# Writing the software loops of a two-block transformer kernel out in straight lines

## The chip, the cores and the metric

One NeuronCore of one Trainium2 chip runs the whole program. The metric is the device time of one execution in microseconds (us), taken without a profile; beside it there is one profiled execution, whose trace the rows below come from.

## What is computed

The program computes a stack of three transformer blocks for one sequence of 256 tokens with model width 1024, in float32: one block with sliding-window, forgetting and latent attention and a convolved feed-forward, then two blocks (`DEPTH_2 = 2`) with adaptive modulation, one with stick-breaking and block attention and one with retention, and a final norm. The change touches how the feed-forward parts, and a few loads around them, are written. In the reference they are

```python
h = rmsnorm(x, ffn_pre_norm[l])
u = causal_depthwise_conv(h @ w_up[l], conv_w[l], conv_b[l])
gate, up = jnp.split(u, 2, axis=-1)
y = (jax.nn.gelu(gate, approximate=True) * up) @ w_down[l]
...
def ada_mod(c, w, b):
    m = jax.nn.silu(c) @ w + b
    return jnp.split(m[:, None, :], 6, axis=-1)
```

The two later blocks have the same feed-forward with silu in place of gelu and without the convolution. `ada_mod` multiplies one vector by a matrix of 1024 x 6144 in each of them; the kernel does this on VectorE.

## The kernel before

All weights come from HBM in chunks of mostly 1 MB, in the order in which TensorE needs them: 171 chunks in twelve phases. The feed-forward phases are `up` (22 chunks), `down` (11), `gu0` (22), `dn0` (16), `gu1` (22) and `dn1` (16). Each engine runs its own hand-written instruction stream, and the streams meet only at semaphores.

A chunk passes through five engines. SyncE (SP) loads it into one of four `raw` slots (L623), once `split_ready` says that the slot's last chunk was split. ScalarE (ACT) writes its high part `w_hi` (L775) and VectorE (DVE) the rest `w_lo` (L2123), two slots each, in two halves. TensorE (PE) then multiplies both parts with both parts of the activations: three matmuls for each 128 x 128 tile of weights (L1409, L1410, L1411 in `three`), so 48 matmuls of 256 columns for a chunk of `up`, `gu0` or `gu1`, and 33 for one of `dn0` or `dn1`. The products of a chunk go to one of two PSUM banks (`lin`). VectorE empties it: in `up` with the four convolution taps of a chunk (L2420), in `gu0` and `gu1` with the product of gate and up (L2444), and only then does `lin_free` let TensorE start the next chunk but one. ScalarE takes the gelu or silu before that and rounds the product afterwards (L1089), and GpSimd (POOL) makes its low part (L695, L702).

Between the chunks stand the pieces of `ada_mod`: SP loads 1 MB into one of two slots of the arena (L613), and VectorE reduces it in two passes of 128 x 1024 (L2227) and adds the bias (L2230). In `up` every second chunk has such a piece, in `gu0` each of the chunks 4 to 19.

The chunk loops go through `steps(eng, n, lead, tail, body)`. It writes out `lead` chunks, puts as many groups of four (`UNROLL = 4`) as fit into a hardware loop (`eng.Fori`), if there are at least two groups, and writes out the rest. Inside the loop everything that depends on the chunk is computed from the loop's counter: semaphore values, row addresses in HBM, columns of `cols` and `mod`. `Step.n(f)` gives a plain number outside a loop and a register expression in one. The calls give these loops (trips of four chunks):

| engine | loops |
|---|---|
| PE | `up`, `gu0`, `gu1`: 3 trips each, chunks 8 to 19; `dn0`: 3; `dn1`: 2 |
| DVE | `up`, `gu0`: 3 trips each, chunks 8 to 19; `dn0`, `dn1`: 2 each; none in `gu1` |
| ACT | `up`, `gu0`: 3 each; `gu1`, `dn0`, `dn1`: 2 each |
| POOL | `up`: 4 trips; `gu0`, `gu1`: 5 each |
| SP | `up`: 3; `qkv`, `gu0`, `dn0`: 2 each; `ret_in`: 5; `dn1`: 3 |

Of the kernel before, what the change touches and what calls it, by code (L numbers as in the profile page):

```python
# [39 lines left out]
UNROLL = 4  # L40
# [147 lines left out]

def steps(eng, n, lead, tail, body):

    lead = min(lead, n)
    trips = (n - lead - tail) // UNROLL
    if trips < 2:
        trips = 0
    for c in range(lead):
        body(Step(c))
    if trips:
        with eng.Fori(0, trips) as i:
            for j in range(UNROLL):
                body(Step(lead + j, i))  # L200
    for c in range(lead + trips * UNROLL, n):
        body(Step(c))


# [81 lines left out]
def build(nc, dram):  # L286
    ctx = ExitStack()
    with ctx:
# [311 lines left out]
        def _(sp):  # L600
# [25 lines left out]
            def phase(ph):  # L626
                load = weights_of(ph)

                def one(step):
                    load(step)  # L630
                    if ph.name == "w_in" and step.j == 1:
                        sp.dma_start(cond_silu, dram["cond"]).then_inc(cond_in, 16)
                    if ph.name == "w_in" and step.j == 2:
                        sp.dma_start(arena[:, TAB1_AT:TAB1_AT + dram["tab1"].shape[1]], dram["tab1"]).then_inc(tab1_in, 16)
                    if ph.name == "up" and step.i is None and step.j == 5:
                        sp.wait_ge(h_tiles, tiles_before(FFNPRE))
                        sp.dma_start(arena[:, TAB2_AT:TAB2_AT + dram["tab2"].shape[1]], dram["tab2"]).then_inc(tab2_in, 16)
                    if ph.name == "gu1" and step.j == 9:
                        sp.wait_ge(h_tiles, tiles_before(FINAL))
                        sp.wait_ge(ada_out, ada_before("gu1", 0))  # L640
                        sp.dma_start(cond_silu, dram["cond"]).then_inc(cond_in, 16)
                    late = 0 if ph.name == "w_in" else ADA_LATE
                    for m in range(ada_here(ph.name, step.j - late) if step.j >= late else 0):
                        load_ada(step, lambda c, m=m: ada_before(ph.name, c - late) + m)

                steps(sp, ph.n, *{"up": (10, 0), "gu0": (12, 1), "dn0": (6, 0), "gu1": (18, 0)}.get(ph.name, (4, 0)), one)
                for c in (ph.n - 2, ph.n - 1) if ph.name != "w_in" else ():
                    for m in range(ada_here(ph.name, c)):
                        load_ada(Step(c), lambda c, m=m: ada_before(ph.name, c) + m)
# [19 lines left out]
        def _(pool):  # L669
# [55 lines left out]
            for i in range(len(NORM_GROUPS)):  # L725
                if i != PRE and NORM_GROUPS[i]:
                    add_squares(i)
                if i in DEFERRED:
                    settle(i)
                if i in (L0F, L1F):  # L730

                    steps(pool, FT, 2, 0, remainder(FT if i == L0F else 2 * FT))
                if i == L1:

                    for h in range(RET_H):
                        pool.wait_ge(ret_sq, 2 * h + 2)
                        nc.gpsimd.tensor_tensor(rt["sq"][:, 0:512], rt["sq"][:, 0:512], rt["sq"][:, 512:1024], ALU.add)\
                            .then_inc(ret_added, 1)
                if i == FFNPRE:

                    steps(pool, PH["up"].n, 2, 1, hidden)
                if i == FINAL:
                    pool.wait_ge(x_gains, DT)
                    pool.wait_ge(rbc_copied, len(DEFERRED) + 1)
                    for k in range(FINAL_SPLIT, DT):
                        cut = slice(k * S, (k + 1) * S)
                        nc.gpsimd.tensor_tensor(e0["y"][:, cut], e0["y"][:, cut], e0["sq"][:, 0:S], ALU.mult).then_inc(pool_tiles, 1)
# [2256 lines left out]
```

## Time and profile before

| | |
|---|---|
| time, three runs | 1065.62, 1066.32, 1067.10 us; median 1066.32 us |
| profiled execution | span 1064.2 us from its first to its last instruction; its own total time is not given apart |
| TensorE busy | 1036.8 us, 97% of the span |
| VectorE, ScalarE, GpSimd busy | 807.3, 592.1 and 156.9 us |
| DMA | 227.27 MB, 214 GB/s on average |

The median of the runs lies 2.1 us above the span of the profiled execution. TensorE's records overlap, since its matmuls are pipelined: a record of a matmul with 256 columns lasts 0.28 us, and the next one starts 0.12 us after it. Time that TensorE loses shows as idle time only where it exceeds that overlap.

### The profile page before, as it was taken

The page shows a single profiled execution, that of the slowest core. Times are in us where ns is not written, and L with a number is a line of the kernel's source. Part 1 is how long each engine was busy: PE and PEld are TensorE (multiplying, and loading weights), DVE is VectorE, ACT ScalarE, POOL GpSimd, SP SyncE. Part 2 cuts the span into 40 slices and gives each one's busy share as a digit, 9 for nine tenths or more (in the row PEclk, how much of TensorE's full clock was granted, in tenths as well). Part 3 has the DMA queues.
Part 4 walks back from the last instruction along what each step waited for, and adds up shares of the span by engine and source line. Part 5 has one row for each costly group of instructions (what it writes and reads, how often), then busy time and mean ns, then how long its engine had stood idle before and what let it go on. Part 6 is the DMA issues. An engine that isn't in the chain of part 4 may idle for free.

```text
span 1064.2 us, 20324 instructions
## 1 busy us (share of the span) xinstructions
PE 1036.8 (97%) x7897; PEld 984.4 (93%) x7897; DVE 807.3 (76%) x1387; ACT 592.1 (56%) x1024; POOL 156.9 (15%) x164
## 2 busy tenths in 40 slices
PE   7999999999999999999999999999999999999998
PEld 6987798999888997899999999998899999999997
DVE  5867689999998997588999788885558667675453
ACT  6686467666536675575444455533466456544443
POOL 0000033333201200024111111200000113111010
PEclk8999999999999999999999999999999999999999
DMA  9642245776696434156998788545334545773451
GB/s 372 239 159 80 79 152 199 287 291 257 254 398 251 159 126 152 55 223 266 363 360 338 263 319 307 196 165 191 119 124 154 201 156 215 255 301 135 168 172 40
DMA packets 33974, 227.27 MB, mean 214 GB/s; under 512 B 3780, under 2 KB 4077, under 8 KB 10221
## 3 DMA queue, kind: packets, MB, share of 16 engines
q1 hardware_dynamic: 33452, 223.63, 56.7%
q0 software_dynamic: 448, 2.63, 0.6%
q8 instruction: 50, 0.82, 0.3%
q14 instruction: 24, 0.19, 0.0%
HBM read 225.19 MB, written 2.63 MB: 214 GB/s over the span
## 4 chain that ended last, share of the span: by engine, by line
PE 74%; DVE 17%; ACT 5%; issue 3%; DMA 1%; DVEq 0%; POOL 0%; ACTq 0%; SPq 0%; POOLq 0%
PE psum L1409 18%; PE psum L1411 17%; PE psum L1410 17%; DVE w_lo L2123 6%; DVE arena L2227 4%; PE psum L1781 3%; PE psum L1783 3%; PE psum L1782 3%; PE psum L1474 2%; PE psum L1477 2%; PE psum L1476 2%; ACT w_hi L775 2%; DVE arena L2380 1%; DVE hid_lo L2208 1%; PE psum L1506 1%
## 5 line engine op out<-in xcount | busy, mean ns | idle before, releaser
L2123 DVE TENSOR_TENSOR w_lo<-raw,w_hi 128x1024 fp32r<-128x1024 f32 (+1 forms) x342 | 389.4, 1162 | 148.7 <-ACT w_hi L775 141.9
L775 ACT ACTIVATE w_hi<-raw 128x1024 fp32r<-128x1024 f32 (+1 forms) x342 | 335.5, 997 | 213.7 <-PE psum L1411 158.8
L1409 PE MATMUL psum<-h_hi,w_hi 128*128 128x256 f32 (+1 forms) x1144 | 327.2, 286 | 9.1 <-DVE w_lo L2123 3.1
L1410 PE MATMUL psum<-h_lo,w_hi 128*128 128x256 f32 (+1 forms) x1144 | 321.4, 281 | 0.0
L1411 PE MATMUL psum<-h_hi,w_lo 128*128 128x256 f32 (+1 forms) x1144 | 320.6, 280 | 0.0
L1409 PE MATMUL psum<-hid_hi,w_hi 128*128 128x256 f32 (+1 forms) x952 | 271.0, 285 | 0.6 <-DVE w_lo L2123 0.4
L1411 PE MATMUL psum<-hid_hi,w_lo 128*128 128x256 f32 (+1 forms) x952 | 268.7, 282 | 0.0
L1410 PE MATMUL psum<-hid_lo,w_hi 128*128 128x256 f32 (+1 forms) x952 | 268.5, 282 | 0.0
L1409 PEld LDWEIGHTS psum<-h_hi,w_hi 128*128 128x128 f32 x1144 | 215.2, 188 | 14.1 <-DVE w_lo L2123 5.5
L1410 PEld LDWEIGHTS psum<-h_lo,w_hi 128*128 128x128 f32 x1144 | 216.2, 189 | 0.7 <-issue 0.7
L1411 PEld LDWEIGHTS psum<-h_hi,w_lo 128*128 128x128 f32 x1144 | 216.0, 189 | 0.0
L1409 PEld LDWEIGHTS psum<-hid_hi,w_hi 128*128 128x128 f32 x952 | 179.7, 189 | 2.3 <-DVE w_lo L2123 1.2
L1410 PEld LDWEIGHTS psum<-hid_lo,w_hi 128*128 128x128 f32 x952 | 179.5, 189 | 0.0
L1411 PEld LDWEIGHTS psum<-hid_hi,w_lo 128*128 128x128 f32 x952 | 179.5, 188 | 0.0
L2227 DVE CUSTOM_DVE_ANT_0 arena<-arena 128x1024 f32<-128x1024 f32 x96 | 128.6, 1377 | 1.7 <-DMA arena<-in_ada 1.5
L682 POOL TENSOR_TENSOR arena<-arena 128x256 f32<-128x256 f32 x33 | 29.4, 891 | 432.9 <-ACT arena L1198 256.7
L1089 ACT ACTIVATE hid_hi<-arena 128x256 f32 (+1 forms) x60 | 25.1, 418 | 103.6 <-DVE arena L2444 78.9
L702 POOL TENSOR_TENSOR hid_lo<-arena,hid_hi 128x256 f32 (+1 forms) x44 | 38.1, 865 | 176.3 <-ACT hid_hi L1089 163.9
L1781 PE MATMUL psum<-w_hi,hid_hi 128*128 128x512 f32 x120 | 47.7, 398 | 1.6 <-DVE hid_lo L2174 1.6
L722 POOL TENSOR_TENSOR arena<-arena 128x256 f32<-128x256 f32 x30 | 36.2, 1225 | 77.6 <-ACT arena L987 64.7
L1782 PE MATMUL psum<-w_hi,hid_lo 128*128 128x512 f32 x120 | 47.4, 395 | 0.0
L1783 PE MATMUL psum<-w_lo,hid_hi 128*128 128x512 f32 x120 | 47.4, 395 | 0.0
(272 smaller groups left out, 1185.7 us busy)
## 6 DMA issues: line engine op xcount, KB each, us to landing
arena<-in_ada SPq DMA_DIRECT2D x48, 1024.0 KB, 6.1
raw<-in_gu SPq DMA_DIRECT2D x44, 1024.0 KB, 6.6
raw<-in_ret_in SPq DMA_DIRECT2D x24, 1024.0 KB, 4.8
raw<-in_up SPq DMA_DIRECT2D x22, 1024.0 KB, 4.8
raw<-in_dn SPq DMA_DIRECT2D x32, 704.0 KB, 4.2
raw<-in_qkv SPq DMA_DIRECT2D x12, 1024.0 KB, 5.3
raw<-in_down SPq DMA_DIRECT2D x11, 1024.0 KB, 7.5
raw<-in_ret_o SPq DMA_DIRECT2D x8, 1024.0 KB, 4.8
```

Source lines behind the costliest of these rows:

```text
L682: nc.gpsimd.tensor_tensor(acc, acc, sq[:, k * S:(k + 1) * S], ALU.add).then_inc(sq_added, 1)
L702: nc.gpsimd.tensor_tensor(hid_lo[:, cut], ff["hid"][:, S * (j % 2):S * (j % 2) + S], hid_hi[:, cut].bitcast(F32), ALU.subtract).then_inc(h ...
L722: nc.gpsimd.tensor_tensor(settled_tile(i, c, b), settled_tile(i, c, b), rbc_copy(i), ALU.mult)\
L775: nc.scalar.activation(w_hi[chunk % SPLIT_SLOTS][:, a:b], raw[chunk % RAW_SLOTS][:, a:b], ACT.Copy)\
L1409: nc.tensor.matmul(out, w[0], hc, start=start, stop=False, skip_group_check=True)
L1410: nc.tensor.matmul(out, w[0], lc, start=False, stop=False, skip_group_check=True)
L1411: return nc.tensor.matmul(out, w[1], hc, start=False, stop=stop, skip_group_check=True)
L1781: nc.tensor.matmul(bank[:, :], hid_hi[:, t:t + P], whi[:, w], start=c == 0 and k == 0, stop=False, skip_group_check=True)
L1782: nc.tensor.matmul(bank[:, :], hid_lo[:, t:t + P], whi[:, w], start=False, stop=False, skip_group_check=True)
L1783: ins = nc.tensor.matmul(bank[:, :], hid_hi[:, t:t + P], wlo[:, w], start=False, stop=last and k == 1, skip_group_check=True)
L2123: tt(w_lo[s][:, a:b], raw[chunk % RAW_SLOTS][:, a:b], w_hi[s][:, a:b].bitcast(F32), ALU.subtract)\
L2227: ins = nc.vector.tensor_tensor_reduce(w, w, cond_silu, 1.0, 0.0, ALU.mult, ALU.add, sums[:, b:b + 1])
```

## The change

`steps` loses its loop: every chunk's body is written out with a plain chunk number, on all five engines.

```diff
 def steps(eng, n, lead, tail, body):
 
-    lead = min(lead, n)
-    trips = (n - lead - tail) // UNROLL
-    if trips < 2:
-        trips = 0
-    for c in range(lead):
-        body(Step(c))
-    if trips:
-        with eng.Fori(0, trips) as i:
-            for j in range(UNROLL):
-                body(Step(lead + j, i))
-    for c in range(lead + trips * UNROLL, n):
+    for c in range(n):
         body(Step(c))
```

The order of the work on each engine stays what it was; line numbers behind L198 fall by ten. The instruction streams change in length. TensorE's goes from 5988 matmuls, 50 register operations, 12 branches and 8 moves to 7536 matmuls and two branches. VectorE's goes from 1077 to 1093 rows, ScalarE's from 727 to 697, GpSimd's from 87 to 70, SyncE's from 194 to 115 (a row stands for several equal instructions in succession).

The first place is the end of VectorE's loop in `gu0` and what follows it; the last chunk of a trip and the start of the next. Before, in the loop's body (`REGISTER_ALU` and the `ISA` rows without names are register work, L2122 the semaphore value of the split, L198 the loop itself):

```order
678 L2122 REGISTER_ALU
679 L2123 TENSOR_TENSOR w_lo<-raw,w_hi 128x1024
680 L2122 REGISTER_ALU
681 L2123 TENSOR_TENSOR w_lo<-raw,w_hi 128x1024
682 L2441 REGISTER_ALU
683 L2444 TENSOR_TENSOR arena<-psum,arena 128x256
684 L2227 ISA arena,ada_sums<-arena 128x1024
685 L2227 ISA ada_sums 128x1
686 L2227 ISA arena,ada_sums<-arena 128x1024
687 L2227 ISA ada_sums 128x1
688 L2230 ISA
689 L2230 TENSOR_TENSOR mod<-ada_sums,cols 128x2
690 L198 REGISTER_ALU
691 L198 COMPARE_AND_BRANCH
```

The same chunk and the start of the next one in the changed kernel:

```order
651 L2113 TENSOR_TENSOR w_lo<-raw,w_hi 128x1024 x2
652 L2434 TENSOR_TENSOR arena<-psum,arena 128x256
653 L2217 ISA arena,ada_sums<-arena 128x1024
654 L2217 ISA ada_sums 128x1
655 L2217 ISA arena,ada_sums<-arena 128x1024
656 L2217 ISA ada_sums 128x1
657 L2220 TENSOR_TENSOR mod<-ada_sums,cols 128x2
658 L2113 TENSOR_TENSOR w_lo<-raw,w_hi 128x1024 x2
```

The work is in the same order; the 24 register and branch rows of a trip of four chunks are gone.

The second place is the start of VectorE's loop in `up`, chunk 8, with its four taps on the products in PSUM. Before:

```order
283 L198 UNCONDITIONAL_BRANCH
284 L198 ISA
285 L2123 TENSOR_TENSOR w_lo<-raw,w_hi 128x1024
286 L2122 REGISTER_ALU
287 L2123 TENSOR_TENSOR w_lo<-raw,w_hi 128x1024
288 L2412 ISA
289 L2420 ISA
290 L2420 SCALAR_TENSOR_TENSOR arena<-psum,cols,arena 128x255
291 L2420 ISA
292 L2420 SCALAR_TENSOR_TENSOR arena<-psum,cols,arena 128x255
293 L2419 REGISTER_ALU
294 L2420 ISA
```

A trip of that loop has 37 such register and branch rows. In the changed kernel none is left; the chunk is `w_lo` x2, then the taps.

## Rows read from the trace of the kernel before

**Rows 1.** The page: the span, and busy time of the engines

```profile
span 1064.2 us, 20324 instructions
...
PE 1036.8 (97%) x7897; PEld 984.4 (93%) x7897; DVE 807.3 (76%) x1387; ACT 592.1 (56%) x1024; POOL 156.9 (15%) x164
```

**Rows 2.** Who TensorE waited for: us in total, times, longest us

```profile
PE psum L1409 <- DVE w_lo L2123: 3.5, 6, 1.2
...
PE psum L1409 <- DVE arena L2420: 2.1, 4, 1.2
...
PE psum L1409 <- DVE arena L2444: 1.7, 3, 1.2
```

**Rows 3.** Timeline of TensorE in `up`: start, us, operation, idle time before

```profile
186.78 0.36 PE L1409 MATMUL psum<-h_hi,w_hi 128*128 128x256 f32 x1 [1.25 <-DVE arena L2420]
...
221.26 0.28 PE L1411 MATMUL psum<-h_hi,w_lo 128*128 128x256 f32 x1
221.88 0.39 PE L1409 MATMUL psum<-h_hi,w_hi 128*128 128x256 f32 x1 [0.34 <-DVE arena L2420]
222.10 0.28 PE L1410 MATMUL psum<-h_lo,w_hi 128*128 128x256 f32 x1
...
245.50 0.38 PE L1409 MATMUL psum<-h_hi,w_hi 128*128 128x256 f32 x1 [0.32 <-DVE arena L2420]
...
268.99 0.36 PE L1409 MATMUL psum<-h_hi,w_hi 128*128 128x256 f32 x1 [0.21 <-DVE arena L2420]
```

**Rows 4.** Timeline of TensorE in `gu0`

```profile
508.00 0.36 PE L1409 MATMUL psum<-h_hi,w_hi 128*128 128x256 f32 x1 [1.18 <-DVE arena L2444]
...
542.99 0.39 PE L1409 MATMUL psum<-h_hi,w_hi 128*128 128x256 f32 x1 [0.27 <-DVE arena L2444]
...
566.65 0.38 PE L1409 MATMUL psum<-h_hi,w_hi 128*128 128x256 f32 x1 [0.23 <-DVE arena L2444]
```

**Rows 5.** Stretches: length, busy us and instructions per engine, clock, DMA share, GB/s

```profile
192.00:274.10 82.10, 81.23 (x674) 80.64 (x673) 77.28 (x120) 50.27 (x83) 29.49 (x28) 1.00 0.71 269
511.30:522.60 11.30, 11.30 (x99) 11.30 (x98) 11.04 (x17) 5.17 (x8) 2.05 (x2) 1.00 0.99 375
511.30:599.10 87.80, 87.30 (x722) 86.01 (x721) 78.97 (x114) 38.81 (x63) 15.21 (x16) 1.00 0.87 331
601.00:661.00 60.00, 60.00 (x502) 60.00 (x501) 51.72 (x85) 30.31 (x47) 6.65 (x6) 1.00 0.87 327
889.50:984.00 94.50, 94.50 (x805) 94.50 (x804) 60.29 (x74) 48.97 (x75) 15.74 (x20) 1.00 0.63 230
```

**Rows 6.** Timeline of VectorE in `gu0`, chunks written out: the splits

```profile
505.17 2.35 DVE L2123 TENSOR_TENSOR w_lo<-raw,w_hi 128x1024 fp32r<-128x1024 f32 x2
...
510.79 2.35 DVE L2123 TENSOR_TENSOR w_lo<-raw,w_hi 128x1024 fp32r<-128x1024 f32 x2
```

**Rows 7.** The same in the loop: start, us, operation, idle time before

```profile
516.53 2.36 DVE L2123 TENSOR_TENSOR w_lo<-raw,w_hi 128x1024 fp32r<-128x1024 f32 x2
...
528.05 0.16 DVE L2230 TENSOR_TENSOR mod<-ada_sums,cols 128x2 f32 x1 [0.18 <-DVE ada_sums L2227]
528.16 2.36 DVE L2123 TENSOR_TENSOR w_lo<-raw,w_hi 128x1024 fp32r<-128x1024 f32 x2
...
540.24 2.36 DVE L2123 TENSOR_TENSOR w_lo<-raw,w_hi 128x1024 fp32r<-128x1024 f32 x2 [0.41 <-issue]
```

**Rows 8.** Who VectorE waited for: us in total, times, longest us

```profile
DVE w_lo L2123 <- issue: 1.7, 5, 0.4
```

**Rows 9.** Timeline of VectorE in `up`, end of the first trip

```profile
216.94 0.16 DVE L2230 TENSOR_TENSOR mod<-ada_sums,cols 128x2 f32 x1 [0.18 <-DVE ada_sums L2227]
217.36 2.90 DVE L2123 TENSOR_TENSOR w_lo<-raw,w_hi 128x1024 fp32r<-128x1024 f32 x2 [0.26 <-issue]
```

**Rows 10.** DMA queues of the whole execution: packets, MB, share of 16 engines

```profile
q8 instruction: 50, 0.82, 0.3%
```

**Rows 11.** DMA issues from 505 to 506 us: KB, us to landing

```profile
arena<-in_ada SPq DMA_DIRECT2D x1, 1024.0 KB, 5.6
```

## The prediction

> **What bounds the kernel now.** I read the page first: TensorE is busy for 1036.8 of 1064.2 us [rows 1]. So no change to the other engines can give much more than TensorE's own pauses, and the question is which pauses come from loops. Next comes the list of what TensorE waited for. Three entries belong to chunk work: 3.5 us for `w_lo`, 2.1 us for the taps L2420 in `up`, 1.7 us for the product L2444 in `gu0` [rows 2]. All three are waits for VectorE. Then the timeline shows where they lie. In `up` the pauses for L2420 are at 186.78, 221.88, 245.50 and 268.99 us [rows 3]; the last three are 23.6 and 23.5 us apart, one trip of four chunks. In `gu0` those for L2444 are at 508.00, 542.99 and 566.65 us [rows 4], the last two again one trip (23.66 us) apart. So some of the pauses beat with the loop, and others (186.78, 508.00) lie in chunks that are written out already and stay.
>
> TensorE's pace tells the rest. A window counts two or three matmuls that are under way at its start, so 889.5 to 984.0 us, in `gu1`, holds some 803 in 94.5 us: 117.7 ns each, 5.65 us for a chunk of 48 [rows 5]. This stretch holds TensorE's own loop with its two back-branches, and its busy time is 94.50 of 94.50 us. TensorE's loop therefore costs nothing by itself. In `gu0`, 511.3 to 522.6 us runs at the same 5.65 us per chunk, but 511.3 to 599.1 us takes 87.8 us for 720 matmuls, 121.9 ns each. The granted clock is 1.00 in all of these, so that is no matter of the clock.
>
> **What VectorE does there.** In `gu0` it is as heavily loaded as TensorE: two halves of `w_lo`, a product, a piece of `ada_mod`. Written out, a chunk takes it 5.62 us (510.79 minus 505.17) [rows 6]. In the loop it is (528.16 - 516.53) / 2 = 5.81 us in the first half of a trip; across the whole trip 540.24 - 516.53 = 23.71 us [rows 7], against 4 x 5.62 = 22.48 us. The difference of 1.23 us has two places: 0.18 us before each addition to `mod`, whose column address has to be computed (four times, 0.72 us), and 0.41 us marked "issue" before the first split of the next trip, where nothing in the trace is waited for and where the loop's branch stands in the instruction order. VectorE has five such "issue" waits before the split, 1.7 us together [rows 8]: two back-branches in `up`, two in `gu0`, one in `dn0`.
>
> By the Trainium skill ("Advanced Engine Details and Errata", Control Flow Timing) a compare-and-branch costs about 108 ns, a quarter of the 0.41 us in the row. With that figure a trip of `gu0` would lose 0.72 + 0.11 = 0.83 us instead of 1.13; the measurement decides, and the sum below does not use it.
>
> **The change, part by part.**
>
> *The loop in `gu0`.* Without register work VectorE needs 5.62 us a chunk, 0.03 us less than TensorE's 5.65. TensorE then no longer waits from the chunk behind 508.00 us on, and its 720 matmuls from 511.3 to 599.1 us run at the pace which the first 96 of them have now: 15 x 5.65 = 84.75 instead of 87.8 us. Gain 3.0 us. A second way to it from VectorE's side: 23.71 - 4 x 5.65 = 1.11 us for each of three trips, 3.3 us. I take 3.0, as TensorE's stretch includes everything.
>
> *The loop in `up`.* Here VectorE has some slack, since only every second chunk carries a piece, and it loses it at the end of each trip: 0.18 us before `mod` and 0.26 us of "issue" behind it [rows 9]. TensorE's pauses of 0.34, 0.32 and 0.21 us follow [rows 3]. A pause costs more than its idle time: the matmul before it started at 221.26 us, the one after it at 221.88, 0.62 us instead of 0.12, and the next interval is 0.22 instead of 0.12 us. So a pause of g costs g + 0.26 us: 0.87 + 3 x 0.26 = 1.65 us. From the stretch: 14 chunks in 82.1 us [rows 5] are 1.5 us over 14 x 5.76 us, where 5.76 us is 48 x 120 ns, this phase's pace away from the pauses. Gain 1.5 us. All three pauses are smaller than or near the 0.44 us that VectorE gets back ahead of each, so I count them as gone; if the last one stayed, the gain would be 1.1 us.
>
> *Loops in `gu1`, `dn0`, `dn1`.* TensorE is busy 94.5 of 94.5 and 60.0 of 60.0 us there [rows 5]. VectorE, ScalarE and GpSimd lose the same kind of overhead, but wait for TensorE afterwards anyway. Zero. SyncE gets its loads out some 0.2 us earlier per chunk; no split waits for a load in these phases, so this is zero too. So are GpSimd's loops: a remainder (L702) is needed a chunk later.
>
> *What is added.* TensorE gets 1548 more matmuls to fetch. The instruction queue q8 brought 50 blocks in 0.82 MB [rows 10]; in proportion 7536/5988 it will be 63. The 13 more packets took, by 0.3% of 16 engines and 1064 us over 50, about 1 us each on one DMA engine out of 16. The chunks of `gu0` that are written out today stream in this way next to DMA queues that are 99% busy (511.3 to 522.6 us) without a pause. Cost 0; upper bound in the rivals. The other engines' streams keep their length.
>
> **Sum:** 1.5 + 3.0 = 4.5 us off the profiled span, 1064.2 to 1059.7 us. The median of the runs lies 2.1 us above that span; with it, 1066.3 - 4.5 = 1061.8 us.
>
> **The rivals.**
>
> *TensorE's pace settles otherwise.* The same 256-column matmuls run at 117.7 ns in `gu1`, at 120 ns in `up` and `dn0` (about 500 in 60.0 us) with no idle time in any of them [rows 5], and I can't derive from the trace what picks the pace; it tends to change at a pause. If `gu0` continues at 120 ns, its 15 chunks take 86.4 us, and only 1.4 of the 3.0 us are gained: 1063.4 us. If, beside it, `gu1` (20 chunks x 0.11 us) fell to 120 ns as well, the time would be 1065.6 us, no change. In the other direction, `up` and `dn0` at 117.7 ns give 1.5 and 1.2 us more: 1059.1 us.
>
> *Loads become the bound in `gu0`.* A chunk and a piece are 2.10 MB; at 5.65 us that is 371 GB/s, held through 84 us, where it is 331 GB/s on average now. From 511.3 to 522.6 us it was 375 GB/s at 99% share, so nothing is left. A piece is loaded after the piece two before it is summed; it landed after 5.6 us [rows 11] and has about 8.1 us. Against it: the two written-out chunks already show this rate, and landing does not drift there. If landing slipped past 8.1 us, VectorE would fall back to today's 5.85 us a chunk and only `up`'s 1.5 us would be left: 1064.8 us.
>
> *Instruction fetch stops TensorE (slower).* The Trainium skill ("Runtime: NRT & Kernel Launch", Instruction fetch mechanics) says that a block is fetched while the one before it is executed, so that crossing into it is mostly hidden, and no pause in `gu1` speaks against that. As a mechanism of this kernel: a block of q8 holds the instructions of some 120 matmuls (5988 over 50), 14 us at 117.7 ns, and its packet takes about 1 us. If a block came later than its 14 us under the full queues of `gu0`, TensorE would stand. With 1 us for each of the 13 added blocks the time is 1061.8 + 13 = 1074.8 us; it decides from 0.35 us per block on. The written-out chunks at 99% DMA share speak against it.
>
> *Nothing moves.* If the 0.18 and 0.41 us were slack in unprofiled runs (the trace itself might slow register work), the time stays at 1066.3 us.
>
> **Chances.** The forecast as summed, with either pace in the phases other than `gu0`: 0.58. `gu0` at the slower pace: 0.12, mostly still faster. Loads bound `gu0`: 0.08. Pace losses cancel the gain or nothing moves: 0.14. Fetch or something else makes it slower: 0.08. A measurement of this kernel tells about 0.2% (2.1 us) from no change, so faster means below 1064.2 us: 0.58 + 0.12 + a little of the loads case, 0.72. Same 0.20, slower 0.08. The range takes in the faster pace in `up` and `dn0` at its lower end and, above, the slow pace in `gu0` and the case where only `up` gains: 1058.8 to 1065.0 us.
>
> **What would show it.** Right: no "issue" waits before `w_lo` on VectorE and no 0.18 us before `mod`; VectorE's splits in `gu0` 5.65 us apart; no pause of TensorE for L2434 (L2444 before) behind the one near 508 us and none for L2410 (L2420 before) behind the one near 187 us; `gu0` 3 us and `up` 1.5 us shorter, `dn0` to `dn1` the same length; q8 with about 63 packets. Wrong: a pace of 120 ns in `gu0` or `gu1`, VectorE waiting for `in_ada`, or TensorE pauses marked "issue" every 120 matmuls.

## The result

| | before | changed |
|---|---|---|
| median | 1066.34 us (1065.62 to 1067.10, 4 runs) | 1061.57 us (1060.33 to 1062.47, 4 runs) |
| profiled execution: its time, its span | not given, 1064.2 us | 1060.33 us, 1058.5 us |

The ratio is 0.9957, 95% interval 0.9946 to 0.9969: 0.43% faster. The forecast was 1061.8 us. The span fell by 5.7 us, the medians by 4.8 us. In five more runs of the changed program the median was 1061.29 us (ratio 0.9959, 0.9945 to 0.9972). A second trace of each kernel, shown further below, has spans of 1063.8 and 1060.0 us, only 3.8 us apart; what makes the spans of one program differ is answered there too.

The page of the changed kernel, answering to [rows 1] and [rows 10]: the span, and the instruction queue that grew.

```profile
span 1058.5 us, 19264 instructions
...
PE 1031.9 (97%) x7897; PEld 982.2 (93%) x7897; DVE 803.9 (76%) x1387; ACT 591.7 (56%) x1024; POOL 156.2 (15%) x164
...
q8 instruction: 62, 1.02, 0.4%
```

The work is the same 7897 matmuls; 1060 records fewer are register operations and branches. What TensorE waited for (us in total, times, longest) answers to [rows 2]:

```profile
PE psum L1399 <- DVE w_lo L2113: 3.3, 6, 1.2
...
PE psum L1399 <- DVE arena L2434: 1.2, 1, 1.2
PE psum L1399 <- DVE arena L2410: 1.2, 1, 1.2
```

Where `up` had four waits for the taps and `gu0` three for the product, one is left in each. The timeline puts them at the two places that are written out in both kernels:

```profile
186.63 0.35 PE L1399 MATMUL psum<-h_hi,w_hi 128*128 128x256 f32 x1 [1.17 <-DVE arena L2410]
...
505.72 0.36 PE L1399 MATMUL psum<-h_hi,w_hi 128*128 128x256 f32 x1 [1.19 <-DVE arena L2434]
```

VectorE in `gu0` (timeline; start, us) keeps 5.62 us from split to split, as it did before its loop began [rows 6]; nothing stands before `mod`, and nothing every fourth chunk, where [rows 7] had 0.18 and 0.41 us:

```profile
519.77 2.35 DVE L2113 TENSOR_TENSOR w_lo<-raw,w_hi 128x1024 fp32r<-128x1024 f32 x2
525.33 0.16 DVE L2220 TENSOR_TENSOR mod<-ada_sums,cols 128x2 f32<-128x2 f32 x1
525.40 2.35 DVE L2113 TENSOR_TENSOR w_lo<-raw,w_hi 128x1024 fp32r<-128x1024 f32 x2
...
531.02 2.35 DVE L2113 TENSOR_TENSOR w_lo<-raw,w_hi 128x1024 fp32r<-128x1024 f32 x2
...
536.65 2.35 DVE L2113 TENSOR_TENSOR w_lo<-raw,w_hi 128x1024 fp32r<-128x1024 f32 x2
...
542.27 2.35 DVE L2113 TENSOR_TENSOR w_lo<-raw,w_hi 128x1024 fp32r<-128x1024 f32 x2
```

The stretches answer to [rows 5]: the part of `up` behind its pause, `gu0` behind its pause with the first 6 us of `dn0`, the rest of `dn0`, `gu1`. (The stretch from 511.3 to 599.1 us in [rows 5] holds 3.2 us of `dn0` in the same way, as `gu0` ends at 595.9 us there.)

```profile
191.90:272.40 80.50, 80.50 (x673) 80.50 (x673) 74.81 (x120) 50.07 (x83) 26.23 (x28) 1.00 0.74 274
509.00:596.70 87.70, 87.70 (x747) 87.70 (x746) 81.17 (x118) 39.82 (x64) 17.85 (x16) 1.00 0.89 334
596.70:655.00 58.30, 58.30 (x493) 58.30 (x493) 50.29 (x84) 30.24 (x47) 5.47 (x6) 1.00 0.88 335
889.50:984.00 94.50, 94.50 (x805) 94.50 (x804) 58.47 (x73) 47.09 (x72) 15.92 (x19) 1.00 0.65 233
```

TensorE is busy all the time in each of them. In the 87.7 us of the second one it starts 745 matmuls, where it started 720 in 87.8 us before.

**Stage by stage.** Every trace holds the same matmuls in the same order, so a stage can be measured from the start of one matmul to the start of a later one, whatever happened ahead of it. From here on `up` means its chunks 7 to 20, the 14 behind the pause at 187 us; `gu0` means its chunks 7 to 21, the last 15, behind the pause at 506 to 508 us, with the first 48 matmuls of `dn0`. Both count from the first matmul behind the pause, and each is worked out from the timeline. TensorE's pace is the time from the start of one matmul to the start of the next:

| us | `up` | `up`'s last chunk, `down`, start of the next norm | `gu0` | `dn0` (480 matmuls) | `gu1` |
|---|---|---|---|---|---|
| before | 82.21 | 80.29 | 93.64 | 57.60 | 126.18 |
| before, second trace | 81.83 | 80.13 | 93.64 | 57.60 | 126.18 |
| changed | 80.69 | 79.80 | 90.58 | 56.96 | 126.18 |
| changed, second trace | 80.69 | 79.79 | 90.58 | 56.96 | 126.18 |

The gain of the first pair is 1.52 + 0.49 + 3.06 + 0.64 = 5.71 us. The 15 chunks of `gu0` alone go from 87.88 to 84.88 us; the other 0.06 us are `dn0`'s.

### The profile page after: what moved, and what is told of

It is laid out like the page before. It is cut to its first block, busy times and chain, and to the rows that moved or that the text cites. A ratio compares the mean times of both kernels' runs of the same rounds, so it can differ in the third digit from the quotient of the medians.

```text
span 1058.5 us, 19264 instructions
## 1 busy us (share of the span) xinstructions
PE 1031.9 (97%) x7897; PEld 982.2 (93%) x7897; DVE 803.9 (76%) x1387; ACT 591.7 (56%) x1024; POOL 156.2 (15%) x164
## 4 chain that ended last, share of the span: by engine, by line
PE 82%; DVE 11%; ACT 5%; issue 1%; DMA 0%; POOL 0%; SPq 0%; POOLq 0%; ACTq 0%; DVEq 0%
PE psum L1399 20%; PE psum L1400 20%; PE psum L1401 20%; DVE w_lo L2113 4%; PE psum L1771 3%; PE psum L1773 3%; PE psum L1772 3%; PE psum L1464 2%; PE psum L1467 2%; PE psum L1466 2%; ACT w_hi L765 2%; DVE arena L2370 1%; DVE arena L2217 1%; DVE hid_lo L2198 1%; PE psum L1496 1%
## 5 line engine op out<-in xcount | busy, mean ns | idle before, releaser
L1079 ACT ACTIVATE hid_hi<-arena 128x256 fp32r<-128x256 f32 x60 | 25.1, 418 | 100.0 <-DVE arena L2434 75.0
L692 POOL TENSOR_TENSOR hid_lo<-arena,hid_hi 128x256 fp32r<-128x256 f32 x44 | 41.8, 951 | 169.2 <-ACT hid_hi L1079 157.1
```

The lines of the kernel that those rows point to most:

```text
L692: nc.gpsimd.tensor_tensor(hid_lo[:, cut], ff["hid"][:, S * (j % 2):S * (j % 2) + S], hid_hi[:, cut].bitcast(F32), ALU.subtract).then_inc(h ...
```

## The experiments

All are timed against the kernel before on the same chip. Its medians there: 1066.23 us for the first three kernels below and the one that moves the pieces of `gu0`; 1065.50 us for the loops put back in one phase, the loop of one trip and the kernel with `dn0`'s loads first; 1065.87 us for the fixed column and the two traces again. `looped` is the old `steps`; the first three edits are shortened to the calls that change.

**Only VectorE written out.**

```diff
-steps(sp, ...)  steps(pool, ...)  steps(act, ...)  steps(pe, ...)
+looped(sp, ...)  looped(pool, ...)  looped(act, ...)  looped(pe, ...)
```

> Only VectorE's chunk loops are written out; SyncE, GpSimd, ScalarE and TensorE keep theirs as before. Theory (VectorE's register work and back-branches are the whole cost): the time of the full change, 1061.6 us, and no TensorE pause behind those near 187 and 506 us. Rival (the other engines' loops cost too, ScalarE's or SyncE's above all): a part of the gain is missing, 1063 to 1065 us.

Measured: 1061.14 us, ratio 0.9963 (0.9948 to 0.9977). `up` takes 80.69 us and `gu0` 90.58 us, to the hundredth what they take in the changed kernel, with four engines still in their loops. One small part of the gain is missing: `up`'s last chunk with `down` takes 80.16 us, as before, and not 79.80. The queue q8 brings 50 blocks:

```profile
q8 instruction: 50, 0.82, 0.3%
```

**Everything but VectorE written out.**

```diff
-steps(dve, ...)
+looped(dve, ...)
```

> The reverse: everything is written out but VectorE's loops. Theory: the time of before, 1066.3 us less what the pace in dn0 gives (up to 0.7 us), with TensorE's pauses one trip apart in up and gu0. Rival (the other engines' loops cost too): 1063 to 1065 us.

Measured: 1064.96 us, ratio 0.9988 (0.9979 to 0.9997). TensorE's pauses are back behind the trips:

```profile
221.82 0.36 PE L1415 MATMUL psum<-h_hi,w_hi 128*128 128x256 f32 x1 [0.54 <-DVE arena L2426]
...
245.20 0.36 PE L1415 MATMUL psum<-h_hi,w_hi 128*128 128x256 f32 x1 [0.53 <-DVE arena L2426]
...
541.79 0.35 PE L1415 MATMUL psum<-h_hi,w_hi 128*128 128x256 f32 x1 [0.30 <-DVE arena L2450]
...
565.46 0.35 PE L1415 MATMUL psum<-h_hi,w_hi 128*128 128x256 f32 x1 [0.36 <-DVE arena L2450]
```

`gu0` takes 93.57 us, all of the 3 us lost. The 1.3 us by which the time still beats the kernel before have several sources in the trace. `dn0` takes 56.96 us and not 57.60, and TensorE never waits in it. `up` (81.18 us) runs its first ten chunks at TensorE's quicker pace, and its third pause, the one at the loop's exit, is missing. The column with `down` is 0.49 us shorter, of which 0.33 us are waits of TensorE at 346 us, between `down` and the next norm. GpSimd and VectorE there, in the kernel before:

```profile
345.32 2.48 POOL L682 TENSOR_TENSOR arena<-arena 128x256 f32<-128x256 f32 x3 [0.51 <-POOL arena L682]
...
345.41 0.92 DVE L2208 SCALAR_TENSOR_TENSOR hid_lo<-x,gscale,hid_hi 128x256 fp32r<-128x256 f32 x1
```

GpSimd's fourth addition starts 0.37 us later than in the written-out kernels, and VectorE's operation that starts just behind it takes 0.92 and not 0.57 us. This stands in both traces of before and in the kernel with only VectorE written out, and in none of the ten others, so it goes with the loops of SyncE, GpSimd and ScalarE taken together; no loop runs at that place, and why the addition comes late stays open. So the theory holds for `gu0`, but not all of the rest is pace.

**Everything but TensorE written out.**

```diff
-steps(pe, ...)
+looped(pe, ...)
```

> Everything is written out but TensorE's five loops, so its instruction queue brings 50 blocks and not 62. Theory (fetching is hidden, and its own loop is free): 1061.6 us, within 0.1%. Rival (the added blocks cost time that the change pays): lower, by up to 12 us if each block costs 1 us. Rival (its own loop costs): higher than 1061.6 us.

Measured: 1059.30 us (1058.74 to 1061.57), ratio 0.9942 (0.9929 to 0.9955). This is below the changed kernel, and at first sight the rival's side. The stages say otherwise: `gu0`, where TensorE's loop has three trips, takes 90.57 us against 90.58; `gu1`, again three trips, 126.19 against 126.18. The difference lies in `up`, 79.22 against 80.69 us, and it begins behind the pause at 187 us, one chunk before the loop. (`ret_o`, in which TensorE has no loop, took 0.71 us longer here, at 120 ns.) The window of the same 80.5 us as above shows ten matmuls more:

```profile
191.90:272.40 80.50, 80.50 (x683) 80.40 (x682) 76.32 (x122) 50.52 (x84) 27.03 (x28) 1.00 0.72 274
```

This is pace, 117.7 and not 120 ns a matmul. That fetching is free in `gu0` and `gu1` is shown by the stages; the 12 blocks cost nothing that can be seen.

**VectorE's loop in `up` alone, and in `gu0` alone.**

```diff
-            steps(dve, ph.n, 8, 1, up_step)
+            looped(dve, ph.n, 8, 1, up_step)
```

> The changed kernel with VectorE's loop put back in up alone. Theory: TensorE's three pauses one trip apart come back there (0.34, 0.32, 0.21 us idle) and cost 1.5 us; gu0 stays as in the changed kernel: 1063.1 us. In the trace, where the pace of single stretches can be taken out: up 1.5 us longer, gu0 the same. Rival (VectorE's slack in up absorbs the loop once the other engines' loops are gone): 1061.6 us, no such pauses.

Measured: 1063.78 us, ratio 0.9977 (0.9966 to 0.9988). `up` takes 81.77 us, 1.08 us more than at the same pace without a loop. Two pauses are back; the third, at the loop's exit, is not, as in the kernel with everything but VectorE written out:

```profile
222.09 0.36 PE L1415 MATMUL psum<-h_hi,w_hi 128*128 128x256 f32 x1 [0.33 <-DVE arena L2426]
...
245.66 0.36 PE L1415 MATMUL psum<-h_hi,w_hi 128*128 128x256 f32 x1 [0.31 <-DVE arena L2426]
```

What makes such a pause shows at the loop's exit, in VectorE's split of two halves and GpSimd's product beside it. First the kernel before, where TensorE's third pause follows:

```profile
264.38 2.90 DVE L2123 TENSOR_TENSOR w_lo<-raw,w_hi 128x1024 fp32r<-128x1024 f32 x2
...
265.40 0.80 POOL L692 TENSOR_TENSOR arena<-arena 128x256 f32<-128x256 f32 x1 [2.50 <-ACT arena L1078]
```

Then the kernel with everything but VectorE written out, where no pause follows:

```profile
263.94 2.36 DVE L2129 TENSOR_TENSOR w_lo<-raw,w_hi 128x1024 fp32r<-128x1024 f32 x2
...
265.09 1.81 POOL L698 TENSOR_TENSOR arena<-arena 128x256 f32<-128x256 f32 x1 [3.76 <-ACT arena L1084]
```

Where GpSimd's product starts before the second half of the split (265.40 against 265.52 us), that half takes 1.76 and not 1.22 us. Where it starts behind it (265.09 against 265.08 us), the half keeps its 1.22 us and GpSimd's product takes 1.81 us. The four traces with VectorE's loop in `up` have ten long halves and ten pauses of TensorE behind the trips, each pause behind a long half; in the nine others no half in `up` is long. So what VectorE loses in the loop itself (0.44 us at the end of a trip) is not the whole loss: it lets GpSimd's product go first, and that costs VectorE 0.54 us more. No kernel here moves GpSimd's product alone, so this rests on the ten cases.

The trace of the kernel with the loop in `up` alone ran `gu0`, which has no loop of VectorE there, at the slower pace: 92.20 us. With `dn0` at 57.60 us that is 2.3 us in which the loop in `up` has no part, so the median does not measure that loop.

```diff
-                steps(dve, ph.n, 14 if ph.name == "gu1" else 8, 2, one)
+                looped(dve, ph.n, 14 if ph.name == "gu1" else 8, 2, one)
```

> The changed kernel with VectorE's loop put back in gu0 alone. Theory: gu0 takes 3.0 us more, 1064.6 us, with TensorE's pauses 23.7 us apart; up stays. Rival (half of it came from other engines' loops): 1063 us.

Measured: 1063.13 us, ratio 0.9977 (0.9967 to 0.9986). `gu0` takes 93.23 us, 2.65 us more than written out, and `up` 79.22 us, at the quicker pace. The time is 1.5 us lower than expected for `up`'s pace alone, a thing this kernel did not touch. In `gu0` TensorE started at the slower pace, at which the kernel above and the next one take 92.2 us without a loop there; against those the loop costs 1.0 us. Two short pauses are back, one trip (23.5 us) apart: 0.41 and 0.40 us between two starts in place of 0.12.

```profile
539.73 0.28 PE L1417 MATMUL psum<-h_hi,w_lo 128*128 128x256 f32 x1
540.14 0.35 PE L1415 MATMUL psum<-h_hi,w_hi 128*128 128x256 f32 x1
...
563.28 0.28 PE L1417 MATMUL psum<-h_hi,w_lo 128*128 128x256 f32 x1
563.68 0.35 PE L1415 MATMUL psum<-h_hi,w_hi 128*128 128x256 f32 x1
```

**A loop of one trip in `gu0`.**

```diff
+def one_trip(eng, n, lead, tail, body):
+    ...
+    with eng.Fori(0, 1) as i:
+        for j in range(count):
+            body(Step(lead + j, i))
```

> VectorE's twelve looped chunks of gu0 as a loop of one single trip: the register work stays, no branch back is ever taken. Theory (0.18 us a chunk for the column of mod, 0.41 us for each of two branches back): VectorE needs 5.62 + 0.18 = 5.80 us a chunk against TensorE's 5.65, so gu0 takes 12 x 0.15 = 1.8 us more: 1063.4 us. Rival (the branches are the whole cost, the register work hides beside the queue): 1061.6 us. Rival (the register work is all of it): 1064.6 us.

Measured: 1061.27 us (1058.75 to 1062.96), ratio 0.9952 (0.9938 to 0.9965). The question was not put: with a counter that can only be zero, the register expressions were resolved to constants when the kernel was built, and what remained was a branch in and out. VectorE's chunks are 5.62 us apart there, with 0.13 us more at the exit. `gu0` took 92.22 us, and 92.20 us in the trace above that had no loop of VectorE there and the same pace. So at this pace, where VectorE has 0.14 us to spare in each chunk, TensorE sees nothing of entering and leaving a loop. The next kernel asks the question again.

**The register work without the column of `mod`.**

```diff
+                if step.i is not None:
+                    tt(spare_mod[:, 0:2], sums, cols[:, o:o + 2], ALU.add).then_inc(ada_out, 1)
+                    return
                 tt(mod[:, bass.ds(step.n(lambda c: 2 * f(c)), 2)], ...
```

> As the kernel with VectorE's loop back in gu0 alone, but the twelve pieces inside the loop write their two sums to one fixed spare column and read one fixed column of the bias, so that no register stands in that instruction (the modulation values of these pieces are left out of mod, which starts as zeros). It splits the loop's cost, since the loop of one single trip was resolved to constants when it was built and held no register work. Theory (0.18 us a chunk for the column, 0.3 to 0.4 us for a branch back): VectorE takes 5.62 us a chunk inside a trip and 22.9 us from trip to trip, not 23.6; the rows before mod show no 0.18 us; gu0 takes 1 us more than written out, against 2.65 us with both. Rival (the 0.18 us only hides the branch's other work and moves elsewhere in the trip): 23.6 us from trip to trip still.

Measured: 1062.21 us (nine runs), ratio 0.9968 (0.9959 to 0.9978). The timeline of VectorE, one trip:

```profile
515.42 2.36 DVE L2130 TENSOR_TENSOR w_lo<-raw,w_hi 128x1024 fp32r<-128x1024 f32 x2
520.98 0.16 DVE L2238 TENSOR_TENSOR spare_mod<-ada_sums,cols 128x2 f32<-128x2 f32 x1
521.08 2.36 DVE L2130 TENSOR_TENSOR w_lo<-raw,w_hi 128x1024 fp32r<-128x1024 f32 x2
...
538.34 2.36 DVE L2130 TENSOR_TENSOR w_lo<-raw,w_hi 128x1024 fp32r<-128x1024 f32 x2 [0.25 <-issue]
```

From trip to trip it is 538.34 - 515.42 = 22.92 us. The kernel to compare it with is the one with VectorE's loop back in `gu0` alone, which differs in the column only:

```profile
513.75 2.36 DVE L2129 TENSOR_TENSOR w_lo<-raw,w_hi 128x1024 fp32r<-128x1024 f32 x2
...
537.30 1.23 DVE L2129 TENSOR_TENSOR w_lo<-raw,w_hi 128x1024 fp32r<-128x1024 f32 x1 [0.26 <-issue]
```

That is 23.55 us, so the column costs 0.63 us a trip, 0.16 us a chunk. Inside a trip the chunks are 5.65 us apart (521.08 - 515.42 = 5.66), 0.03 us over the 5.62 of the written-out ones: the other register operations of a chunk, most of which run while VectorE is still busy, cost 0.12 us a trip. The rest, 22.92 - 4 x 5.65 = 0.32 us, is the branch back. The forecast of 22.9 us came true, with the 5.62 us inside a trip missed by that 0.03.

The branch has no fixed price. The same loop over `gu0` showed 0.41 and 0.39 us of "issue" in the kernel before, in both its traces, and in the kernel with all of VectorE's loops, but 0.26 and 0.24 us where it is VectorE's only loop. The 23.71 us of [rows 7] are thus 4 x 5.62 + 0.64 for the column + 0.12 for other register work + 0.47 for the branch. Why the same branch costs more in one kernel than in another stays open. TensorE had the slower pace in this trace (`gu0` 92.07 us), so that its 5.76 us a chunk hid even the branches; what they cost at the quicker pace was not seen.

**The two traces again.**

> The changed kernel once more, for its trace. Question: is TensorE's pace (117.7 or 120 ns a matmul) a matter of the program or of the single execution? Theory (of the execution): in one stretch or more (up, gu0, dn0, ret_o) the pace differs from the first trace of the same program, and the run times stand 1.5 to 2.5 us apart in groups. Rival (of the program): all stretches as in the first trace, within 0.1 us.

> The kernel before once more, for its trace: the same question of the pace. The pauses behind the loop's trips (0.34, 0.32, 0.21 us in up; 0.27, 0.23 us in gu0) come back at the same places if they are the loop's; if the pace is of the execution, one of the stretches differs by 1 us or more. Rival: the trace repeats within 0.1 us.

Measured: 1061.29 us (1060.22 to 1061.90) for the changed kernel; one run of 1065.62 us for the one before. The stages are in the table above: all of the changed kernel's repeat within 0.01 us, and both traces of before have 93.64 and 57.60 us. `up` differs by 0.38 us in the kernel before: its pauses for L2420 are 0.33, 0.54 and 0.43 us in the second trace, where [rows 3] have 0.34, 0.32 and 0.21. Between them TensorE was quicker. The window 224 to 244 us, behind the first of these pauses, in the first and then in the second trace of before:

```profile
224.00:244.00 20.00, 20.00 (x169) 20.00 (x168) 18.42 (x30) 12.09 (x20) 7.45 (x8) 1.00 0.69 272
```

```profile
224.00:244.00 20.00, 20.00 (x172) 20.00 (x171) 18.63 (x30) 12.15 (x21) 7.65 (x8) 1.00 0.70 280
```

One program, with 120 ns a matmul there in one execution and 117.7 ns in the other, from the first loop pause on. So the pace is not fixed by the program. For the kernel before, the expectation was wrong in its size (no stretch differs by 1 us), and its rival, a repeat within 0.1 us, failed as well. For the changed kernel the rival held in all the stages of the table.

The spans of the two traces of the changed kernel differ by 1.5 us, and the difference arises ahead of `up`. The largest piece, 1.4 us, lies between 97 and 102 us, where the granted clock was 1.00 in the first trace (2.4 GHz) and went down to 0.50 (1.2 GHz) in the second. The window 97 to 100 us in the first and then in the second:

```profile
97.00:100.00 3.00, 2.98 (x29) 2.36 (x28) 2.19 (x14) 2.97 (x11) 0.00 (x0) 1.00 0.62 194
```

```profile
97.00:100.00 3.00, 3.00 (x19) 2.33 (x17) 1.77 (x11) 2.72 (x10) 0.00 (x0) 0.55 0.55 153
```

So executions of one program can differ by 1.4 us for this reason alone, nearly as much as the whole loop in `up` costs. The first trace of the kernel before had the low clock there too, so the 5.7 us between the first two spans hold 1.4 us of clock; the changed kernel's trace lost 1.2 us of it again in the first 25 us, where its clock was low for longer.

**Moving the pieces of `gu0`.** TensorE's two remaining pauses there lie where VectorE takes on its first pieces right behind the norm.

```diff
-("gu0", 22, lambda c: int(4 <= c <= 19))
+("gu0", 22, lambda c: int(6 <= c <= 21))
```

> The changed kernel with the sixteen pieces of gu0 at chunks 6 to 21, not 4 to 19; the work is the same. Theory: TensorE's two remaining pauses in gu0 (0.92 us for w_lo at 498.5 us, 1.19 us for the product at 505.7 us) come from VectorE taking on pieces while it still catches up from the norm; without them both go, 0.92 + 1.19 + 2 x 0.26 = 2.6 us: 1059.0 us. Rival (VectorE has no reserve against TensorE at 5.62 to 5.65 us a chunk, so the pauses only move to chunk 6): 1061.6 us. Rival (two more pieces meet the start of dn0 and its loads): slower than 1061.6 us.

Measured: 1060.03 us, ratio 0.9943 (0.9930 to 0.9956), half of what was hoped. The two pauses went: the 96 matmuls that end with the second one take 11.31 instead of 13.92 us, 2.6 us as forecast. The same 2.6 us come back at the other end. Timelines of TensorE and of SyncE's queue:

```profile
588.30 0.36 PE L1399 MATMUL psum<-hid_hi,w_hi 128*128 128x256 f32 x1 [0.91 <-DVE arena L2434]
...
593.91 0.36 PE L1399 MATMUL psum<-hid_hi,w_hi 128*128 128x256 f32 x1 [1.45 <-DVE w_lo L2113]
...
566.79 11.57 SPq L603 DMA_DIRECT2D arena<-in_ada  x3
578.41 2.23 SPq L613 DMA_DIRECT2D raw<-in_dn  x4
```

Two loads of late pieces stand in SyncE's queue ahead of the first load of `dn0`. Each waits until VectorE has finished the piece two before it, and the first chunk of `dn0` goes out only at 578.41 us.

**The same with `dn0`'s loads first.**

```diff
+                    if ph.name == "dn0" and step.j < 2:
+                        load_ada(Step(20 + step.j), lambda c: ada_before("gu0", c))
...
-                for c in (ph.n - 2, ph.n - 1) if ph.name != "w_in" else ():
+                for c in (ph.n - 2, ph.n - 1) if ph.name not in ("w_in", "gu0") else ():
```

> As the kernel with the pieces at chunks 6 to 21 of gu0, but SyncE issues the first two chunks of dn0 each ahead of the load of a late piece, which waits for VectorE. In the earlier trace the first load of dn0 stood behind two such waits, went out at 578.4 us and landed 6.8 us later, and TensorE paused for 0.91 and 1.45 us at the start of dn0. Theory (that queue is the whole of it): those pauses go, 0.91 + 1.45 + 2 x 0.26 = 2.9 us less than that kernel with the same pace elsewhere, 1058 us in the middle. Rival (VectorE itself is late with the two pieces, at 583 and 591 us): TensorE still pauses there, 1060 us.

Measured: 1057.54 us (1056.36 to 1059.16), ratio 0.9923 (0.9910 to 0.9936), the quickest of all. SyncE's queue:

```profile
567.08 0.33 SPq L603 DMA_DIRECT2D arena<-in_ada  x1
567.45 0.43 SPq L613 DMA_DIRECT2D raw<-in_dn  x1
572.71 0.33 SPq L603 DMA_DIRECT2D arena<-in_ada  x1
573.08 0.43 SPq L613 DMA_DIRECT2D raw<-in_dn  x1
```

The first chunk of `dn0` goes out 11 us earlier, `gu0` takes 90.72 us and not 93.33, and no wait of TensorE for L2434 or its like is left in `gu0` or at the start of `dn0`. VectorE has the two late pieces in the same order as in the kernel before this one, so it was the queue and not VectorE.

## Why the prediction was right

*TensorE bounds, and some of its pauses beat with VectorE's loop.* Shown. With VectorE alone written out the gain of `up` and `gu0` is complete; with VectorE alone looped, `gu0` has none of it.

*The total.* 1061.57 us against 1061.8 is closer than the method is: the changed kernel's own runs lie 2.1 us apart, and the stages gain 5.7 us in the first pair of traces and 5.2 in the second, where the medians fell by 4.8 and 4.6 us. That part of the agreement is luck.

*`gu0`, 3.0 us.* Measured 3.06 us between the traces, 3.00 us for its 15 chunks. The mechanism is the one given: VectorE at 5.62 us a chunk just keeps ahead of TensorE at 5.65 (the sign that was forecast, VectorE's splits 5.65 us apart, was off by these 0.03). Its two terms, 0.18 us a chunk for the column of `mod` and 0.41 us for a branch back, were separated by the fixed column, in a kernel where a branch shows 0.25 us: 0.63 us a trip for the column, forecast at 0.72, and 0.32 us for the branch. The missing 0.1 us of the 1.23 is the other register work. As for the branch, 108 ns (the Trainium skill, "Advanced Engine Details and Errata", Control Flow Timing) stays below what a taken branch really loses, 0.23 to 0.41 us of "issue" at each in `up` and `gu0`; where the branch is not taken, at the loops' exits, the idle time is 0.03 us. The "issue" includes the register operation behind the branch, and no kernel here takes that out.

*`up`, 1.5 us.* Measured 1.52 us between the traces, 1.08 us with the loop put back alone, 1.14 us between the second pair. That VectorE's loop makes the pauses was right. What the forecast had wrong is how: it put the pauses down to the 0.44 us that VectorE loses at the end of a trip, but at each of them the next split also takes 0.54 us longer beside GpSimd's product (2.90 us in [rows 9], where 2.36 is usual). At the loop's exit VectorE loses only 0.21 us, and the pause comes or stays away with these 0.54 us. So the agreement in size is partly luck. (The up row in [rows 5] is not free of idle time either, as the rival on pace says: 81.23 of 82.10 us busy.)

*Zero for `dn0`, `gu1`, `dn1` and for the other engines' loops.* `gu1` and `dn1` are unchanged to 0.02 us. `dn0` got 0.64 us shorter without a pause in either trace (57.60 and 56.96 us for 480 matmuls, 120 and 118.7 ns). That is pace, the rival that the forecast priced at 1.2 us for `dn0` in that direction. The column with `down` got 0.49 us shorter: 0.33 us of it go with GpSimd's late addition, which stands only where SyncE, GpSimd and ScalarE have their loops and which the forecast had at zero; the other 0.16 us are not there in the second pair of traces. Together these make up nearly all of the 1.2 us by which the span's gain exceeds the forecast of 4.5 us.

*Zero for fetching.* Shown in the stages of the kernel with TensorE's loops back: 50 blocks or 62, `gu0` and `gu1` take the same time to 0.01 us. By the Trainium skill ("Runtime: NRT & Kernel Launch", Instruction fetch mechanics) crossing into a block is mostly hidden, and the traces agree.

*The rival on loads.* It came as near as it could. In the changed kernel the DMA from 530 to 560 us ran at this (the window's totals, and its issues with KB and us to landing):

```profile
q1 hardware_dynamic: 1538, 11.28, 99.2%
...
arena<-in_ada SPq DMA_DIRECT2D x6, 1024.0 KB, 5.2
raw<-in_gu SPq DMA_DIRECT2D x6, 1024.0 KB, 7.6
```

The queues stay at 96% or more of their engines' time from 505 to 575 us, at 366 to 393 GB/s, and yet a piece lands after some 5.2 us with 8 us to go. Landing did not drift (4.9 to 5.5 us in stretches of 15 us). Full queues over 70 us were no bound here.

*The rival on pace in `gu0`* did not happen in either trace of the changed kernel, but it did in three related ones: 92.20, 92.22 and 92.07 us, 1.6 us over 90.58, as priced (86.4 instead of 84.75 us for 15 chunks; measured 86.44 and 84.88). A pair of windows of 40 us, the changed kernel and then the one with VectorE's loop in `up`, both with VectorE's `gu0` written out and no pause:

```profile
520.00:560.00 40.00, 40.00 (x342) 40.00 (x342) 39.76 (x57) 18.10 (x28) 8.41 (x7) 1.00 0.99 375
```

```profile
526.00:566.00 40.00, 40.00 (x335) 40.00 (x335) 39.76 (x58) 18.68 (x30) 8.39 (x7) 1.00 0.98 376
```

What picks the pace stays open, but not when. The granted clock is 1.00 at both. In `up` and `gu0` it changes only behind a delay, and a short one is enough: where TensorE never stalls, all 14 or 15 chunks have one pace, and in `gu0` of the kernel before it goes to and fro between 117.8 and 120.0 ns from chunk to chunk, each time behind a delay at the chunk's start (0.13 to 0.55 us between two starts, where 0.12 is usual). In `up` the 14 chunks take 80.69 us in the changed kernel, twice, and in three others, 79.2 us in four others, and the two kinds part right behind the pause at 187 us. The length of the pause does not decide it (1.17 us went with either). The program does not decide it alone either, as the two traces of before show. That every other stretch kept its pace in both repeats is no proof against it: there are only two pairs. The groups in the run times (1058.75, 1059.18 and 1060.12 us against 1062.41, 1062.91 and 1062.96 us for the loop of one trip) can come from the pace or from the clock in the first 100 us; no run here separates these.

## What to carry to other kernels

Look whether the pauses of the engine that bounds the kernel come at the loop's period; the loop that matters is then that of the engine which it waits for, and writing out that one alone brought nearly all of the gain here. Its price is for the most part not the instructions in the loop but those that stand in the open, an address that the last result needs and the branch, and it only counts on an engine with little reserve per trip. A small delay can cost more than itself when it puts an operation behind one of another engine: compare the length of the same operation in every trip. A load that waits for a compute engine holds everything behind it in the same DMA queue: put loads that the next stage needs ahead of it.

## What the runs showed of the hardware

TensorE had more than one pace with matmuls of the same shape, a granted clock of 1.00 and no idle time: 117.7 and 120 ns a matmul, with 118.7 ns in `dn0`. It is worth 1.5 us over 14 chunks, as much as the whole loop in `up`, and it differs between the traces of kernels that differ in nothing but VectorE's code in another phase. It was settled anew behind delays of TensorE, short ones too, and once differently in two executions of one program. Differences of 1 to 2 us between such kernels were to be read from the stages of the trace, not from the medians.

VectorE's split and GpSimd's product did not run side by side at full speed in `up`: the one that started second took longer (VectorE's half 1.76 in place of 1.22 us, GpSimd's product up to 1.81 in place of 0.74).

A taken branch back on VectorE showed 0.23 to 0.41 us of idle time, one that is not taken 0.03 us; a computed column cost 0.16 us.

A loop of a single trip carried no register work in its chunks, since its counter is known when the kernel is built, and so cannot stand in for a loop.
